# One value page to three key pages and five value quads behind the second softmax, in a four-layer hybrid decoder step

## The reference

```python
gate = jnp.einsum('blhd,bnhd->blhn', q, block_mean)
gate = jnp.where(eligible[None, :, None, :], gate, -jnp.inf)
_, sel = lax.top_k(gate, k_sel)                       # three past blocks, and the own one
s = jnp.einsum('bqhd,bqhkld->bqhkl', qg, kg).astype(jnp.float32) * scale
s = jnp.where(mask, s, -jnp.inf).reshape(b, qb, H, n_slots * MOBA_BLOCK)
p = jax.nn.softmax(s, axis=-1).reshape(b, qb, H, n_slots, MOBA_BLOCK)
return jnp.einsum('bqhkl,bqhkld->bqhd', p, vg)        # then @ w_o

u = jnp.sqrt(-jnp.expm1(2.0 * log_a)) * (i * x_br)    # RG-LRU: h = a * h + u, token by token
y = jax.nn.gelu(gate_br) * hs                         # then @ w_out

y = y.reshape(b, L, SSD_D_INNER) * jax.nn.silu(z)     # SSD, at its end
y = rmsnorm(y.reshape(b, L, SSD_GROUPS, -1), ...)     # by group, then @ w_out
```

## Time and profile before

| what | value |
|---|---|
| median of 3 executions | 1928.94 us (1928.9 to 1932.74) |
| the profiled execution | 1931.62 us, its span 1930.0 us |
| busy: TensorE, VectorE, ScalarE, GpSimd | 1768.6, 1312.6, 954.5, 506.9 us |
| chain that ended last: TensorE, VectorE, ScalarE | 69, 15, 7 % of the span |
| HBM traffic | 340.79 MB read, 23.15 MB written |

### The profile page before, as it was taken

How to read it: one execution, slowest core, us unless ns; L and a number is a source line. 1 busy time by engine, 2 the same in 40 slices (tenths; PEclk the granted TensorE clock), 3 DMA queues, 4 the chain that set the end, 5 groups by cost and what they waited for, 6 DMA issues and landing times.

```text
span 1930.0 us, 35670 instructions
## 1 busy us (share of the span) xinstructions
PE 1768.6 (92%) x13463; PEld 1639.6 (85%) x13463; DVE 1312.6 (68%) x2450; ACT 954.5 (49%) x1730; POOL 506.9 (26%) x442
## 2 busy tenths in 40 slices
PE   8999989999999474899999979999999998999998
PEld 6998759999998332599999969999899875999997
DVE  6989895555576878465557875554899879655555
ACT  4456753553345755355434645533554675445333
POOL 2601401441121334154212124411160050144111
PEclk9999989999999777999999989999999998999999
DMA  7555574655567799765555436545446448365550
GB/s 214 152 175 159 142 230 138 206 188 176 174 228 271 283 383 398 254 208 185 175 174 156 153 114 209 187 158 177 153 136 192 137 135 262 113 206 190 178 174 23
DMA packets 317604, 365.05 MB, mean 189 GB/s; under 512 B 7738, under 2 KB 290562, under 8 KB 317382
## 3 DMA queue, kind: packets, MB, share of 16 engines
q1 hardware_dynamic: 296356, 288.46, 47.6%
q0 software_dynamic: 20944, 74.84, 10.5%
q10 hardware_dynamic: 176, 0.09, 0.0%
HBM read 340.79 MB, written 23.15 MB: 189 GB/s over the span
## 4 chain that ended last, share of the span: by engine, by line
PE 69%; DVE 15%; ACT 7%; issue 3%; DVEq 2%; DMA 2%; POOLq 1%; POOL 1%; ACTq 0%; SPq 0%
PE G L562 20%; PE G L563 20%; PE G L564 19%; DVE wlo L1753 5%; ACT whi L1080 3%; DVE sums L2078 2%; PE A L1016 2%; DVE xbc L1926 1%; PE A L523 1%; PE A L889 1%; ACT raw L1253 1%; DVEq L1928 1%; PE G L768 1%; DVE stx L2070 1%; PE G L686 1%
## 5 line engine op out<-in xcount | busy, mean ns | idle before, releaser
L1753 DVE TENSOR_TENSOR wlo<-raw,whi 128x2048 fp32r<-128x2048 f32 x234 | 549.0, 2346 | 327.1 <-ACT whi L1080 326.9
L1080 ACT ACTIVATE whi<-raw 128x2048 fp32r<-128x2048 f32 x234 | 447.9, 1914 | 546.2 <-PE G L564 542.0
L562 PE MATMUL G<-xH,whi 128*128 128x264 f32 x2112 | 606.1, 287 | 14.3 <-DVE wlo L1753 11.7
L563 PE MATMUL G<-xH,wlo 128*128 128x264 f32 x2112 | 600.6, 284 | 0.0
L564 PE MATMUL G<-xL,whi 128*128 128x264 f32 x2112 | 600.2, 284 | 0.0
L562 PEld LDWEIGHTS G<-xH,whi 128*128 128x128 f32 x2112 | 399.8, 189 | 24.6 <-DVE wlo L1753 12.1
L563 PEld LDWEIGHTS G<-xH,wlo 128*128 128x128 f32 x2112 | 400.1, 189 | 0.4 <-issue 0.2
L564 PEld LDWEIGHTS G<-xL,whi 128*128 128x128 f32 x2112 | 398.3, 189 | 0.0
L562 PE MATMUL G<-aH,whi 128*128 128x264 f32 x1024 | 292.2, 285 | 8.0 <-DVE wlo L1753 8.0
L564 PE MATMUL G<-aL,whi 128*128 128x264 f32 x1024 | 290.7, 284 | 0.0
L563 PE MATMUL G<-aH,wlo 128*128 128x264 f32 x1024 | 290.7, 284 | 0.0
(11 more groups left out here) (464 smaller groups left out, 3022.3 us busy)
## 6 DMA issues: line engine op xcount, KB each, us to landing
raw<-in_mlp_w_up SPq DMA_DIRECT2D x64, 1024.0 KB, 5.3
raw<-in_mlp_w_down SPq DMA_DIRECT2D x64, 1024.0 KB, 5.1
raw<-in_ssd_w_in SPq DMA_DIRECT2D x48, 1024.0 KB, 5.4
pg<-in_cache_k POOLq DMA_DIRECT2D x64, 512.0 KB, 5.9
raw<-in_ssd_w_out SPq DMA_DIRECT2D x16, 1024.0 KB, 6.9
raw<-in_ple_w_gate SPq DMA_DIRECT2D x16, 1024.0 KB, 5.1
raw<-in_moba_w_qkv SPq DMA_DIRECT2D x12, 1024.0 KB, 7.4
pgw<-in_cache_v POOLq DMA_DIRECT2D x20, 512.0 KB, 6.5
```

The source lines that it names most:

```text
L562: mm(o, whi[u % 2][:, k, w], act_h[:, x, :], start=first, stop=False)
L563: mm(o, wlo[u % 2][:, k, w], act_h[:, x, :], start=False, stop=False)
L1080: fn(whi[u % 2][:], raw[(u + 2) % 4][:], ACT.Copy).then_inc(s_hi, 1)
L1753: V.tensor_tensor(wlo[u % 2][:], raw[(u + 2) % 4][:], whi[u % 2][:].bitcast(F32), ALU.subtract).then_inc(s_lo, 1)
```

## The change

- GpSimd: beside the key pages from t = 24 on, one value page to each three key pages in place of two. Value pages 0 to 2 are issued in the gate stage of layer 0 (`first_pages`), page 3 and pages 12, 13 earlier in qkv. The four first buffers move.
- TensorE: heads 0 to 2 come earlier; `quad(2)` now stands ahead of `query(5)`, `quad(3)` behind `weights_T(4)`, and quads 4 to 8 one after the other behind `shares_T(1)`, the second softmax.
- Heads: the mask is added by TensorE (a product of `past` and a unit matrix in bf16), the copy of keys and values moves from VectorE to ScalarE (`weigh`), and maxima and exponentials read PSUM. The tuples have five heads in the scan.
- qkv: for r = 1 to 3 `qkv_out(r)` stands ahead of `split(r)`. `rows` uses a product with the unit matrix where it had transposes, and writes to partitions 32j.
- SSD: the reciprocal of `grs` moves from k = 7 to k = 6; the L768 products become `root_rows(0)` to `root_rows(3)`, the first ahead of `spread(7)`.
- LRU: on ScalarE `decay(1)` stands ahead of `split(1, 2)`; on VectorE `one_less_square(1)` ahead of `evicted(6)`, `gated(halves[0])` ahead of `evicted(7)`, and `out_low(0, 0)` ahead of the last two `gated`.

```diff
+                def root_rows(j):
+                    for e in range(2):
+                        g = 2 * j + e
+                        t_ = mm(root_bank[j][:, e * SEQ:(e + 1) * SEQ], ident[0:GROUPS, g:g + 1].to_broadcast([GROUPS, P]),
+                                hv2["grs"][:], start=True, stop=True)
+                    t_.then_inc(s_gb, 1)
...
+                    if k == NB - 1:
+                        pe.wait_ge(s_gs, q + 1)
+                        root_rows(0)
                     spread(k)
-                pe.wait_ge(s_gs, q + 1)
+                root_rows(1)
                 pe.wait_ge(s_add, 2 * NB * (q + 1))
-                for g in range(GROUPS):
-                    t_ = mm(bank[4 + g // 2][:, (g % 2) * SEQ:(g % 2 + 1) * SEQ], ident[0:GROUPS, g:g + 1].to_broadcast([GROUPS, P]),
-                            hv2["grs"][:], start=True, stop=True)
-                    if g % 2:
-                        t_.then_inc(s_gb, 1)
+                root_rows(2)
+                root_rows(3)
...
-                        t_ = tr(dst[0:NB, hh // 4, (hh % 4) * P:(hh % 4 + 1) * P], qkv[:, 8 * j + hh, S_], P)
+                        t_ = mm(dst[32 * j:32 * j + NB, hh // 4, (hh % 4) * P:(hh % 4 + 1) * P], qkv[:, 8 * j + hh, S_], ident[:], start=True, stop=True)
...
+                        pe.wait_ge(s_mex, hh)
+                    mm(score_bank[:, 0:P], past[:], identB[:], start=False, stop=True, skip_group_check=True)
+                    mm(score_bank[:, 2 * P:3 * P], past[:], identB[:], start=False, stop=True, skip_group_check=True).then_inc(s_mtp, 1)
...
+                front(0)
+                weights_T(0)
+                head_sum(0)
                 scores_T(0)
                 query(4)
                 shares_T(0)
+                front(1)
                 quad(0)
-                front(0)
+                weights_T(1)
                 quad(1)
+                front(2)
+                head_sum(1)
                 quad(2)
-                front(1)
-                weights_T(0)
-                quad(3)
-                head_sum(0)
                 query(5)
-                weights_T(1)
-                quad(4)
-                head_sum(1)
-                quad(5)
-                front(2)
-                query(6)
                 weights_T(2)
-                quad(6)
                 head_sum(2)
                 front(3)
+                query(6)
+                weights_T(3)
+                head_sum(3)
+                front(4)
                 query(7)
-                weights_T(3)
-                front(4)
-                head_sum(3)
-                quad(7)
                 weights_T(4)
-                scores_T(1)
+                quad(3)
                 head_sum(4)
                 front(5)
+                scores_T(1)
+                weights_T(5)
+                front(6)
                 shares_T(1)
+                head_sum(5)
+                quad(4)
+                quad(5)
+                quad(6)
+                quad(7)
                 quad(8)
-                weights_T(5)
+                weights_T(6)
                 quad(9)
-                head_sum(5)
-                front(6)
+                front(7)
+                head_sum(6)
                 quad(10)
-                weights_T(6)
+                weights_T(7)
                 quad(11)
-                head_sum(6)
-                front(7)
                 gather(0)
+                head_sum(7)
                 quad(12)
-                weights_T(7)
                 quad(13)
-                head_sum(7)
                 quad(14)
                 quad(15)
                 gather(1)
...
+                    fn(mh[f"kvt{b}"][:], kv_bank.rearrange("p (j d) -> p j d", j=4), ACT.Copy)
+                    fn(sc[:, 0:P], score_bank[:, 0:P], ACT.Exp, scale=SCALE, bias=nm[:, 0:1], accum_out=rs[:, 0:1])
+                    fn(sc[:, P:3 * P], score_bank[:, P:3 * P], ACT.Exp, scale=SCALE, bias=nm[:, 1:2], accum_out=rs[:, 1:2]).then_inc(s_mex, 1)
...
+            def first_pages():
                     key_page(0, j)
+                for t in range(3):
+                    value_page(t)
             def moba():
                     key_page(0, j)
-                for k, t in enumerate((0, 1, 2, 3, 12, 13)):
-                        pool.wait_ge(s_mm, qkv["g0"] + 2 + k // 2)
+                for t in (12, 13):
                     value_page(t)
+                pool.wait_ge(s_mm, qkv["g0"] + 2)
+                value_page(3)
...
-                        if (PAGES * (n - 3) + j) % 3 < 2:
+                        if (PAGES * (n - 3) + j) % 3 == 0:
                             value_page(later.pop(0))
...
-                    if k == NB - 1:
+                    if k == NB - 2:
...
-                    if r < 4:
-                        split(st, 0, r)
                     if r == 0:
+                        split(st, 0, 0)
                         rms(3)
                     dve.wait_ge(s_mm, st["g0"] + r + 1)
                     qkv_out(r, (r + st["c0"]) % 2)
+                    if 0 < r < 4:
+                        split(st, 0, r)
...
-                    V.tensor_copy(mh[f"kvt{b}"][:], kv_bank.rearrange("p (j d) -> p j d", j=4))
-                    V.tensor_tensor(sc[:], score_bank[:, 0:3 * P], amask[:], ALU.add)
-                    V.tensor_reduce(mx[:, 0:1], sc[:, 0:P], AX, ALU.max)
-                    V.tensor_reduce(mx[:, 1:2], sc[:, P:3 * P], AX, ALU.max)
+                    mx, nm = mh[f"mx{b}"], mh[f"nm{b}"]
+                    V.tensor_reduce(mx[:, 0:1], score_bank[:, 0:P], AX, ALU.max)
+                    V.tensor_reduce(mx[:, 1:2], score_bank[:, P:3 * P], AX, ALU.max)
...
+                    for hh in range(5):
+                        if t == (20, 35, 39, 47, 55)[hh]:
                             scores(hh)
-                        if t == (37, 41, 49, 57)[hh]:
+                        if t == (22, 37, 41, 49, 57)[hh]:
                             shares(hh)
-                        if t == (43, 45, 53, 60)[hh]:
+                        if t == (28, 42, 46, 53, 61)[hh]:
                             head_out(hh)
...
+                scores(5)
                 block_parts(1)
-                head_out(4)
-                scores(5)
+                shares(5)
                 normalised(1)
                 spread(1)
-                shares(5)
                 ov = ms["ov"][:].rearrange("p (b h) -> p b h", h=MH)
-                for hh in range(6, MH):
-                    head_out(hh - 1)
-                    scores(hh)
-                    shares(hh)
-                    dve.wait_ge(s_vd, 40)
-                    split(stage[1, "qkv"], 2, hh - 4)
+                scores(6)
+                head_out(5)
+                shares(6)
+                scores(7)
+                head_out(6)
...
+                one_less_square(1)
                 evicted(6)
                 split(st, 1, 2)
-                one_less_square(1)
                 scan(0)
+                gated(halves[0])
                 evicted(7)
-                gated(halves[0])
                 scan(1)
+                out_low(0, 0)
                 gated(slice(4, 6))
                 gated(slice(6, 8))
-                for k in (0, 2, 4, 6):
-                    out_low(k, max(0, k // 2 - 1))
+                out_low(2, 0)
+                out_low(4, 1)
+                out_low(6, 2)
...
+                decay(1)
                 split(st, 1, 2)
-                decay(1)
                 one_decay(1)
                 root_of(0)
                 root_of(1)
-                for u in range(4):
+                for u in range(3):
                     gelu(u)
-                for n in range(3):
-                    out_high(n)
+                out_high(0)
+                gelu(3)
+                out_high(1)
+                out_high(2)
```

More of the change, by code:

```diff
@@ L190, in build_trunk @@
         ysp, _ = row(XT * TILE_B, [("yH", [P, XT, T], F32R), ("yL", [P, XT, T], F32R)])
-        M, m1 = row(0, [("qkv", [P, 3 * MH, T]), ("att", [P, KT, T]), ("rowS", [NB, 3, D])])
+        M, m1 = row(0, [("qkv", [P, 3 * MH, T]), ("att", [P, KT, T]), ("spare", [P, 2 * D]), ("rowS", [72, D])])
         pg, m2 = row(m1, [(f"pg{j}", [P, MH, P]) for j in range(PAGES)])
@@ L774, in ssd @@
                 for e in range(2):
-                    t_ = mm(bank[3][:, 0:GROUPS * NB], ones[:], ysv[:, :, e, :], start=(e == 0), stop=(e == 1))
+                    t_ = mm(bank[4][:, 0:GROUPS * NB], ones[:], ysv[:, :, e, :], start=(e == 0), stop=(e == 1))
                 t_.then_inc(s_gv, 1)
@@ L802, in query @@
                         t_ = mm(query_bank(n)[:, c, :], ident[0:NB, n:n + 1].to_broadcast([NB, P]),
-                                M["rowS"][:, 0, c * 512:(c + 1) * 512], start=True, stop=True)
+                                M["rowS"][0:NB, c * 512:(c + 1) * 512], start=True, stop=True)
                     t_.then_inc(s_qbc, 1)
@@ L845, in shares_T @@
                     pe.wait_ge(s_sP, f + 1)
```

(42 more changed lines are left out.)

75 lines of the change are left out of this document (29 added, 46 removed).

## The result

The changed kernel took 1943.43 us (median of 6 runs, 1939.71 to 1948.29), the kernel before 1929.85 in the same runs: a ratio of 1.0069, 95 % interval 1.005 to 1.0088, 13.6 us slower. The forecast was slower by 6.4, 1935.3, with a range of 1925 to 1942. A second measurement of the changed kernel beside the experiments gave 1945.35 against 1930.57, 1.0068 (1.0048 to 1.0088). The sign and the place were right; the forecast has half of the loss.

What follows compares the result with a forecast made beforehand. TensorE, busy 92 % of the span, bounds the dense stages; the change acts where it waits, longest in MoBA. MoBA +12.3, SSD -2.5 and LRU -3.4 give +6.4 on 1928.94, so 1935.3, range 1925 to 1942.

Steps and rivals of the forecast that it cites:

- 0.5 for the first page's products: MoBA's tail: the products of quad 4's first page take 0.5 us before its buffer is free for page 32.
- 0.7 to the issue: MoBA's tail: 0.7 us from the first page's products to GpSimd's issue of page 32.
- wait at page 40: MoBA's scan at t = 40: VectorE stands 7.3 us for query(5), behind quad 2 and value page 11; +6.9.
- the same 6.1 as before: End of MoBA's tail: 6.1 us from the last page's landing to wo, unchanged from the kernel before.
- its 67.8: MoBA's tail from the scan's end to wo: 67.8 us, against 48.0 before.
- net -1.1: qkv: TensorE's 2.12 us wait before rows(0) goes, rows(0) doubles its passes for +1.0; net -1.1 us.
- -2.5: Two SSD layers: the second norm's reciprocal no longer waits 1.25 us for ScalarE, -1.25 in each; -2.5 us.
- -3.4: LRU: the first scan starts earlier and two gate products step back, so TensorE's first output product comes 3.4 us earlier.
- no stall at page 40: Rival, MoBA's scan: page 11 lands in time, so the stall at t = 40 does not come; 1929.2, chance 0.32.
- a light queue: Rival, MoBA: DMA keeps up with GpSimd, the tail is 64.6 and no query comes late; 1922.8, chance 0.18.
- the queue backing up: Rival, MoBA's tail: the last landing takes the 10.8 us of a full queue, tail 72.1; 1939.6, chance 0.07.
- The small edits standing idle: Rival, LRU and SSD: the first product and the norm wait for something else, +5.9 on the forecast; 1941.2, chance 0.05.

Runs made afterwards that it cites:

- two to three: Changed kernel with two value pages to three keys as before and quads 2 to 7 spread over the scan, other edits kept: 1916.48 us, ratio 0.9924 to the kernel before.
- the query ahead: Changed kernel with only query(5) moved back ahead of quad(2): 1939.95 us against 1930.45 for the kernel before, ratio 1.0042.
- the ratio alone: Changed kernel with two value pages to three keys and query(5) ahead of quads 2 and 3, quads 4 to 7 still behind the second softmax: 1941.93 us, ratio 1.0057.
- the small edits alone: Kernel before plus only the edits outside the page attention (qkv's evictions, SSD, LRU): 1921.77 us, ratio 0.9957 to the kernel before.
- the quads ahead: Changed kernel with quad 4 ahead of the second scores and quads 5 and 6 between scores and shares, one value page to three keys: 1931.95 us, ratio 1.0001.

## Why the prediction was wrong in its size

In short: two steps of its sum failed. The tail's "0.5 for the first page's products" and "0.7 to the issue" are 3.1 and 1.4, since the first page ends with its whole quad. And every duration of TensorE was taken at one speed, while its clock was lower with the change. Together they are 12 us in the profiled execution, of which qkv gave 3 back.

**Right: the tail and its cause.** The scan ended at 751.7 (forecast 749.9), GpSimd ran out behind page 31, page 32 came 17.7 us behind the scan (forecast 14.5), the 31 pages took 39.4 (39.4), the landing 7.7 (7.8). DMA is full in the tail (1.03), as the forecast has it; from the issue of page 32 to the last landing it is 47.0 us (47.2). That the 39.4 agrees to the tenth is in part luck, since GpSimd issued 30 times in 36.1 us and then stood 2.74 ahead of the last page. The kernels with the quads at either place show the cause: 25.5 us at two to three, 11.5 to 13.4 at one to three. Not as forecast, DMA did not stand through the whole softmax; it was full until about 761.

**Wrong, first: "0.5 for the first page's products".** Page 32 waits for page 16, the first page of quad 4, and I took a quarter of a quad for it. The four pages of a quad go through TensorE together. In quad 0 three pages lie in pgf and one in sums, and the timeline shows one product of each in a round of 0.85 us, four rounds a quad:

```profile
685.87 1.09 PE L903 MATMUL A<-pgf,pm 128*32 128x512 f32 x3
685.91 1.06 PE L903 MATMUL A<-sums,pm 128*32 128x512 f32 x1
686.73 1.09 PE L903 MATMUL A<-pgf,pm 128*32 128x512 f32 x3
686.77 1.06 PE L903 MATMUL A<-sums,pm 128*32 128x512 f32 x1
```

So the first page is done with the last. Quad 4 begins at 764.95 and quad 5 at 768.04, 3.1 us mostly at the low clock, and page 32 is issued 1.4 us later (769.42): 4.5 in place of 1.2 from quad 4 to the issue, 3.3 us short. In the second trace of the change the clock was full here; quad 4 took 1.7 (766.18 to 767.92) and page 32 followed 1.4 later again (769.29). The two stretches:

```profile
764.95:768.04 3.09, 3.09 (x17) 0.84 (x17) 1.16 (x5) 0.91 (x4) 0.00 (x0) 0.55 0.32 90
```

```profile
766.18:767.92 1.74, 1.74 (x18) 0.58 (x18) 1.01 (x5) 0.91 (x4) 0.00 (x0) 1.00 0.00 0
```

So 1.9 of the 3.3 are this step, and 1.4 the clock. The other traces agree: with the query ahead quad 4 starts at 755.69 and page 32 is issued at 760.31; with the ratio alone at 761.83 and 766.38; the issue comes 1.4 us behind the start of quad 5 in both. The same "0.5, a quarter of a quad" stands in the forecast's wait at page 40. There too the whole quad follows the page, 1.95 at full clock; the page landed sooner than forecast (5.6 us for 6.5), which hid most of it.

**Wrong, second: "the same 6.1 as before", and each duration of TensorE at one speed.** I took 1.98 for a query and 6.1 from the last landing to wo from rows at full clock, and asked nowhere what the change does to the clock. It takes four quads out of TensorE's scan and leaves its waits longer, and the granted clock in the scan fell from 0.68 to 0.58. Over 645 to 750 us it was 0.58 to 0.62 in the five traces with quads 4 to 7 behind the softmax, 0.62 and 0.64 with them around the second scores, and 0.65 to 0.70 in the three with them in the scan (small edits, before, two to three). This bears it out, but the steps are small beside the spread. The low clock costs 3.3 of the 9.4 us at the end of the tail and 3.0 of the 10.5 at page 40. At a later query VectorE waits 3.1 us at the low clock and 1.3 at the full one (forecast 1.2). At the end of the tail the quads' place is not the reason: with the quads ahead wo follows quad 15 by 9.4 too, and with two to three by 7.3. With the first point these are the whole difference of MoBA in the first trace: forecast from qkv's end to wo were 13.4 (12.3 and the 1.1 of qkv), the tail took 6.4 more than its 67.8, the three queries 5.8 more than their 9.7; that makes 25.6, and the table has 25.7.

**Wrong, third, in my favour: qkv "net -1.1".** The scan began 4.2 us earlier by it. The two stretches behind `rows(0)`, before and after:

```profile
590.70:597.20 6.50, 6.50 (x31) 5.16 (x28) 0.71 (x1) 2.70 (x2) 0.00 (x0) 0.74 0.65 222
597.20:606.70 9.50, 9.50 (x54) 8.06 (x53) 6.97 (x26) 4.54 (x18) 1.06 (x2) 0.82 0.53 171
```

```profile
588.60:593.60 5.00, 5.00 (x29) 3.62 (x28) 0.71 (x1) 2.72 (x2) 0.00 (x0) 1.00 0.67 216
593.60:601.50 7.90, 7.90 (x53) 6.51 (x52) 6.92 (x26) 4.48 (x18) 1.06 (x2) 1.00 0.40 119
```

The wait of 2.12 us had been followed by a clock of 0.74 and 0.82; without it the clock stays at full, and the same products take 5.0 and 7.9 us in place of 6.5 and 9.5. So removing the wait gave 1.1 and its clock another 3.0. Without this the scan would have ended at about 755, 5 behind my forecast; that it came out within 2 us is luck.

**SSD, "-2.5": right in its cause, near in its size.** The second norm's reciprocal no longer waits for ScalarE. In the last layer it begins 2.76 us behind the squares, where it was 3.91 before (1634.19 to 1638.10 in its timeline):

```profile
1652.12 0.29 DVE L2108 TENSOR_TENSOR ys<-zs 128x128 f32<-128x128 f32 x1
1654.88 0.54 DVE L2127 RECIPROCAL grn<-grn 128x64 f32<-128x64 f32 x1
```

From the first row spread (L737 before, L738 after) to the first output product the two layers took 61.37 and 62.02 us before, 60.69 and 61.09 with the change, 60.03 and 60.94 with the small edits alone: 0.7 to 1.3 and 0.9 to 1.1 less, against 1.25 each. Of all nine traces with these edits eight agree in the first layer (60.03 to 60.77) and nine in the last (60.38 to 61.16); the second trace of the change has 62.29 in the first, longer than before, and why is open. The table's last two lines have 1.6, 1.7, 0.1 and 2.2 us less between them: the stretch from the MLP to the last mixer, which no edit touches, differs by -1.5 to +1.1 between the traces.

**LRU, "-3.4": right, and partly given back.** The first product came 3.7 earlier, its wait is 10.15 in place of 13.72. The change then lost 1.25 behind it (1.1 in its second trace); the small edits alone lost nothing. The clock tells why (stretches from the first product on, the change, then the small edits alone):

```profile
1140.40:1143.40 3.00, 2.80 (x13) 2.83 (x14) 2.82 (x6) 1.96 (x3) 0.00 (x0) 0.50 0.00 0
1143.40:1146.40 3.00, 3.00 (x15) 3.00 (x15) 2.34 (x2) 1.14 (x1) 0.00 (x0) 0.50 0.02 5
```

```profile
1111.10:1114.10 3.00, 2.80 (x13) 2.83 (x14) 2.81 (x6) 1.96 (x3) 0.00 (x0) 0.50 0.00 0
1114.10:1117.10 3.00, 3.00 (x26) 3.00 (x26) 2.33 (x2) 1.15 (x1) 0.00 (x0) 1.00 0.00 0
```

At the low level for 6 us in the one, for 3 in the other, with the same order of the LRU. What holds it low longer is open.

**Left open.** What decides between the two levels in one execution and the other of the same kernel was not tried. The runs of the change spread over 9 to 11 us (six runs each). Since the tail and page 40 differ with the clock in the traces, I take the clock for the cause, but this was only argued: the four runs with two to three spread over 3, and so do the four with the ratio alone, whose clock is low.

The forecast's rivals: no stall at page 40 and a light queue did not come; the queue backing up is near in its time (1939.6) and not in its reason, since the last page landed in 7.7 us and not 10.8. The small edits standing idle is nearest in its time (1941.2) and falls too: the wait before the LRU's output is 10.15, and the small edits alone gain 8.8 us.

## What to carry to other kernels

When work is moved behind a synchronization point, list which buffers it frees and which transfers wait for them: four quads moved behind one softmax stopped GpSimd's issues for 16 us in the change, and for 31 at two to three, where their place is worth 25.5. Ask of every wait that a change lengthens or removes what the engine behind it does to its clock, and price the next instructions at both levels. And where a product counts a semaphore per part, see in the timeline whether the parts really end one after the other.

## What the runs showed that I had not expected

- Removing a wait of 2.12 us in a dense stage gave 4.2, since TensorE's clock no longer fell behind it (0.74 and 0.82 to 1.00).
- The products of a quad's four pages go into different partition groups and run in rounds, so that all pages end together: 3.1 us mostly at the low clock, 1.7 at the high one, and the waiting issue 1.4 behind in either case.
- The same instructions up to `query(5)` gave waits of 10.5, 10.7, 6.3 and 5.9 us in four traces; 3.0 of the difference are TensorE's clock.
- With idle products between the last quads the clock stayed up (one trace) and the tail's end was 1.5 to 3.3 us shorter, and the time of the whole kernel did not show it.
